# Queries, keys and recurrent inputs of the second mixer turned by transposing DMAs instead of TensorE

## The reference, cut to what matters

```python
def parallel_mixer(h, positions, w_in, conv_w, conv_b, w_rg, b_rg, w_ig, b_ig, lru_lambda, fox_b_f, w_out):
    proj = h @ w_in
    lx, ly, fq, fk, fv, ff, rq, rk, rv, rg = jnp.split(proj, np.cumsum(SPLIT_SIZES)[:-1].tolist(), axis=-1)
    lru_out = rg_lru(causal_depthwise_conv(lx, conv_w, conv_b), w_rg, b_rg, w_ig, b_ig, lru_lambda) * jax.nn.gelu(ly)
    fox_out = forgetting_attention(fq, fk, fv, ff, fox_b_f)
    ret_out = retention(rq, rk, rv, rg, positions)
    return jnp.concatenate([lru_out, fox_out.astype(h.dtype), ret_out], axis=-1) @ w_out

# in forgetting_attention, per head, with scale = HEAD_DIM ** -0.5:
logits = jnp.einsum('bhqd,bhkd->bhqk', qb, k).astype(jnp.float32) * scale + cb[..., None] - c[:, :, None, :]
```

## Time and profile before

| | us |
|---|---|
| runs | 2044.07, 2046.35, 2046.73 (median 2046.35) |
| span of the profiled execution | 2042.2 |
| PE busy | 2021.6 (99%) |
| DVE busy | 1410.4 (69%) |
| ACT busy | 1123.0 (55%) |
| mixer of the second block, layer 0, units 3 to 12 | 1235.6 to 1299.2 in the span |
| the same, layer 1 | 407.8 later |

### The profile page before, as it was taken

One profiled execution on the slowest core, in us unless ns is written; L12 is line 12 of the kernel. 1 busy time (PEld: TensorE's weight loads), 2 busy tenths in 40 slices (PEclk: granted clock), 3 DMA queues, 4 the chain that ended last, 5 costly groups with the idle time before them and its releaser, 6 DMA issues.

```text
span 2042.2 us, 24517 instructions
## 1 busy us (share of the span) xinstructions
PE 2021.6 (99%) x9754; PEld 1669.9 (82%) x9754; DVE 1410.4 (69%) x1855; ACT 1123.0 (55%) x1414; POOL 0.2 (0%) x4
## 2 busy tenths in 40 slices
PE   8999999999999999999999999999999999999998
PEld 6888887888888888887878888898888888988887
DVE  6666898776567556998776566856756658567565
ACT  6445667564445445666564446656544566565443
POOL 0000000000000000000000000000000000000000
PEclk9999999999999999999999999999999999999999
DMA  9776764567776775664567766444667654446764
GB/s 290 201 212 171 237 188 143 185 193 212 206 216 209 206 209 191 205 194 145 180 201 222 207 192 204 146 155 140 188 207 214 184 201 145 160 139 186 209 213 119
DMA packets 330226, 389.31 MB, mean 191 GB/s; under 512 B 102640, under 2 KB 238464, under 8 KB 330112
## 3 DMA queue, kind: packets, MB, share of 16 engines
q1 hardware_dynamic: 326016, 376.70, 60.5%
q10 hardware_dynamic: 4096, 11.05, 1.5%
HBM read 365.66 MB, written 1.05 MB: 180 GB/s over the span
## 4 chain that ended last, share of the span: by engine, by line
PE 95%; ACT 2%; DMA 2%; DVE 1%; issue 0%; SPq 0%; DVEq 0%; ACTq 0%
PE ps L584 85%; PE ps L1088 2%; PE ps L652 1%; PE ps L1191 1%; PE ps L1172 1%; DMA raw<-in_ffn_w_up 1%; PE ps L675 1%; ACT w_hi L1251 1%; PE ps L821 1%; DVE x L1869 0%; DMA raw<-in_w_in 0%; PE ps L1036 0%; PE ps L1002 0%; PE ps L727 0%; ACT scratch L1302 0%
## 5 line engine op out<-in xcount | busy, mean ns | idle before, releaser
L1829 DVE TENSOR_TENSOR w_lo<-raw,w_hi 128x2048 fp32r<-128x2048 f32 x338 | 772.4, 2289 | 268.9 <-ACT w_hi L1251 266.5
L1251 ACT ACTIVATE w_hi<-raw 128x2048 fp32r<-128x2048 f32 x342 | 648.5, 1897 | 458.6 <-PE ps L584 267.6
L584 PE MATMUL ps<-w_hi,hT_hi 128*128 128x512 f32 x2048 | 805.7, 393 | 1.4 <-DVE w_lo L1829 1.4
L584 PE MATMUL ps<-w_lo,hT_hi 128*128 128x512 f32 x2048 | 797.8, 390 | 0.0
L584 PE MATMUL ps<-w_hi,hT_lo 128*128 128x512 f32 x2048 | 775.4, 390 | 0.0
L584 PEld LDWEIGHTS ps<-w_hi,hT_hi 128*128 128x128 f32 x2048 | 384.6, 188 | 84.7 <-issue 5.5
L584 PEld LDWEIGHTS ps<-w_hi,hT_lo 128*128 128x128 f32 x2048 | 383.6, 188 | 79.9
L584 PEld LDWEIGHTS ps<-w_lo,hT_hi 128*128 128x128 f32 x2048 | 384.7, 188 | 76.9
L584 PE MATMUL ps<-w_hi,bT_hi 128*128 128x512 f32 x592 | 232.0, 392 | 0.5 <-DVE bT_lo L1910 0.5
L584 PE MATMUL ps<-w_lo,bT_hi 128*128 128x512 f32 x592 | 230.5, 389 | 0.0
L584 PE MATMUL ps<-w_hi,bT_lo 128*128 128x512 f32 x592 | 230.5, 389 | 0.0
(11 more groups left out here) (292 smaller groups left out, 1288.7 us busy)
## 6 DMA issues: line engine op xcount, KB each, us to landing
raw<-in_w_in SPq DMA_DIRECT2D x160, 512.0 KB, 4.6
raw<-in_ffn_w_gate SPq DMA_DIRECT2D x88, 512.0 KB, 4.0
raw<-in_ffn_w_up SPq DMA_DIRECT2D x88, 512.0 KB, 5.0
raw<-in_ffn_w_down SPq DMA_DIRECT2D x88, 512.0 KB, 4.3
raw<-in_w_gate SPq DMA_DIRECT2D x44, 512.0 KB, 4.0
raw<-in_w_up SPq DMA_DIRECT2D x44, 512.0 KB, 5.0
raw<-in_w_down SPq DMA_DIRECT2D x44, 512.0 KB, 4.2
raw<-in_w_out SPq DMA_DIRECT2D x32, 512.0 KB, 4.4
```

Of the source, the lines that this page charges most:

```text
L584: mm = nc.tensor.matmul(bank(t, half), act[:, tiles[i], t * P:(t + 1) * P], w, start=start and (i, n) == steps[0], stop=stop and (i, n) == ...
L1251: nc.scalar.activation(dst, src, ACT.Copy).then_inc(high_ready, 1)
L1829: V.tensor_tensor(lo, src, flat(hi), ALU.subtract).then_inc(low_ready, 1)
```

## The change

Queries, keys and x/y of the second mixer no longer pass through PE and PSUM. The rows that ACT wrote are split into planes by DVE (`fox_part`, `lru_part`), turned by two transposing DMAs each, and joined by DVE (`fox_join`, and two joins in `lru_conv`). The queries' factor 1/8 moves from ACT's copy into `rstd_eighth`, a small product on DVE. Planes and turned planes lie in tensors that are free at that time (`wide`, the upper half of `fvrT_f`, `vm`); the x/y planes reuse those of the queries. ACT's copies of the turned queries and keys are gone.

```diff
+                    if k == 9:
+                        sp.wait_ge(*after("fox_join", "q_planes", l))
+                        turn_planes(fq_planes_T, fq_planes, fox_q_turned)
+                    if k == 10:
+                        sp.wait_ge(*after("fox_join", "k_planes", l))
+                        turn_planes(fk_planes_T, fk_planes, fox_k_turned)
+                    if k == 12:
+                        sp.wait_ge(*after("lru_turn", "planes", l))
+                        turn_planes(lxy_planes_T, lxy_planes, lru_turned)
...
-        def fox_turn(l, which):
-            pe.wait_ge(*after("fox_in", which, l))
-            if which == "k":
-                pe.wait_ge(*after("fox_gate", "rows", l))
-            turn(fq if which == "q" else fk, 4 if which == "q" else 6).then_inc(*done("fox_turned", which))
-
-        def lru_turn(l):
-            pe.wait_ge(*after("lru_in", "xy", l))
-            pe.wait_ge(*after("fox_in", "qT", l))
-            turn(lxy, 4).then_inc(*done("lru_turned", "xy"))
...
-                pe.wait_ge(*after("fox_in", "kT", l))
+                pe.wait_ge(*after("fox_join", "k", l))
...
-            steps = {(1, 0): [fox_forget], (1, 1): [fox_decay, lambda l: fox_turn(l, "q")],
-                     (2, 1): [lambda l: fox_turn(l, "k")], (3, 1): [lru_turn, lambda l: fox_logits(l, 0)],
+            steps = {(1, 0): [fox_forget], (1, 1): [fox_decay], (3, 1): [lambda l: fox_logits(l, 0)],
...
-                       2: lambda: (act.wait_ge(*after("fox_turned", "q", l)), copy(fqT, two(4), "fox_in", "qT", 64 ** -0.5)),
-                       3: lambda: (act.wait_ge(*after("fox_turned", "k", l)), copy(fkT, two(6), "fox_in", "kT")),
...
+                if n == 0:
+                    act.wait_ge(*after("fox_join", "eighth", l))
+                if n == 4:
+                    act.wait_ge(*after("fox_join", "q", l))
...
+        def fox_part(l, which):
+            dve.wait_ge(*after("fox_in", which, l))
+            part_planes(fq_planes if which == "q" else fk_planes, fq if which == "q" else fk).then_inc(
+                *done("fox_join", which + "_planes"))
+
+        def fox_join(l, which):
+            dve.wait_ge(fox_q_turned if which == "q" else fox_k_turned, l * 32 + 32)
+            join_planes(*((fqT, fq_planes_T) if which == "q" else (fkT, fk_planes_T))).then_inc(*done("fox_join", which))
+
+        def lru_part(l):
+            dve.wait_ge(*after("lru_in", "xy", l))
+            part_planes(lxy_planes, lxy).then_inc(*done("lru_turn", "planes"))
+
         def lru_conv(l):
-            dve.wait_ge(*after("lru_turned", "xy", l))
-            V.tensor_copy(lxT[:, :, PAD2:PAD2 + T], two(4)[:, 0:2, :]).then_inc(*done("lru_turn", "x"))
-            V.tensor_copy(lyT.rearrange("p (c t) -> p c t", c=2), two(4)[:, 2:4, :]).then_inc(*done("lru_turn", "y"))
+            dve.wait_ge(lru_turned, l * 32 + 32)
+            src = lxy_planes_T.rearrange("p t (b c) n -> p t b c n", b=2)
+            join_planes(lxT[:, :, PAD2:PAD2 + T], src[:, :, :, 0:2, :]).then_inc(
+                *done("lru_turn", "x"))
+            join_planes(lyT.rearrange("p (c t) -> p c t", c=2), src[:, :, :, 2:4, :]).then_inc(*done("lru_turn", "y"))
...
+            V.tensor_scalar(rstd_eighth, rstd_in, 0.125, None, ALU.mult).then_inc(*done("fox_join", "eighth"))
             fox_gate(L)
             weight_low(L, 7)
+            fox_part(l, "q")
             fox_sums(l)
             weight_low(L, 8)
+            fox_part(l, "k")
             lru_lambda(l)
-            for k in (9, 10, 11, 12):
-                weight_low(L, k)
+            fox_join(l, "q")
+            weight_low(L, 9)
+            fox_join(l, "k")
+            weight_low(L, 10)
+            lru_part(l)
+            weight_low(L, 11)
+            weight_low(L, 12)
             lru_conv(l)
```

More of the change, by code:

```diff
@@ L300, in _program @@
     lxy = pairbuf.rearrange("p (t n) -> p t n", t=TT)
+    fq_planes, fq_planes_T = planes(wide[:, 0:1024]), planes_T(rT_f)
+    fk_planes, fk_planes_T = (w.rearrange("p m n -> p (m n)") for w in (vm[:, 0:1, :], vm[:, 1:2, :]))
+    fk_planes, fk_planes_T = planes(fk_planes), planes_T(fk_planes_T)
+    lxy_planes, lxy_planes_T = fq_planes, fq_planes_T
     ry_f, rsq_f = pairbuf[:, 0:512], pairbuf[:, 512:1024]
@@ L333, in _program @@
     conv_turned, gla_q_turned, sb_turned = sem("conv_u_turned"), sem("gla_q_turned"), sem("sb_qk_turned")
+    fox_q_turned, fox_k_turned, lru_turned = sem("fox_q_turned"), sem("fox_k_turned"), sem("lru_xy_turned")
     gT_hi_ready, gT_ready = sem("gT_hi_ready"), sem("gT_ready")
@@ L1382, in rows @@
         def rows(dst, src, stage, step, func=ACT.Copy):
-            scale = rstd_half if func == ACT.Tanh or step == "a" else rstd_eighth if (stage, step) == ("sb_in", "q") else rstd_in
+            scale = rstd_half if func == ACT.Tanh or step == "a" else rstd_eighth if step == "q" else rstd_in
             for t in range(TT):
@@ L2003, in join_planes @@
         def join_planes(dst, src):
+            if len(src.shape) == 4:
+                src = src.rearrange("p t (b c) n -> p t b c n", b=2)
             for t in range(TT):
                 joint = V.tensor_copy(dst.bitcast(U16).rearrange("p c (n b) -> p b c n", b=2)[:, :, :, t * P:(t + 1) * P],
-                                      src[:, t, :, :].rearrange("p (b c) n -> p b c n", b=2))
+                                      src[:, t, :, :, :])
             return joint
```

## The result

The changed kernel takes **2058.58 us** (median of 5 runs, 2055.41 to 2059.37), the kernel before 2046.73 in the runs beside it (2044.07 to 2047.78). The ratio is 1.0058, 95% interval 1.0048 to 1.0069: 11.85 us slower, where 10 had been forecast.

The account below looks back on a forecast made before the run. PE, busy 99% of the span, was taken as the bound: 2.6 us of turns spared per layer, but waits and clock loss leave each layer 5.0 us late; 2046.35 + 10 = 2056.4 us, range 2051.5 to 2062.

Parts of the forecast that it names:

- Steps 1 to 3: Layer 0, queries' and keys' splits, transposes and joins: unit 10 lands at 1266.3; first logits don't wait, 3 us spare.
- Step 4: Layer 0: x and y split behind unit 10's w_lo, planes at 1271.7; unit 12's load issued at 1274.4, landing at 1279.7.
- the bound of 6.3: Landings of units 10 and 12: at most 6.3 us, up to 1 us more each than the 5.3 used.
- Step 5: Layer 0: unit 12's w_lo, x and y joins, taps end at 1288.3; PE waits 5.9 us at the gates.
- the bound of twice that: DVE's joins of x and y could cost up to twice their neighbours, writing a padded tensor: 1.4 us more.
- The second wait: At the turned weights: sigmoids end 9.6 us after the last tap, so PE waits 1.3 us more.
- 0.45 us beyond the sigmoids for the clock: Behind the gates' wait: half clock loses PE 1.75 us, of which 1.3 were idle anyway, leaving 0.45 a layer.
- The turns are simply gained: Rival: unit 12's weights and planes come in time, nothing waits, 5.2 us gained, 2041.1 us; chance 0.04.
- The wait only eats the gain: Rival: path some 4 us shorter, PE waits about 2 us, kernel within 4 us of before, say 2048; chance 0.05.
- The milder loss: Rival: clock doesn't fall, landings short; 3.4 to 4 us a layer, 2053 to 2054.5 us; chance 0.15.
- The longer clock loss: Rival: clock stays low longer or falls twice a layer, another 1.75 us each, 2060 us; chance 0.13.
- I am wrong if unit 12's raw weights land before PE ends unit 10: Sign against the forecast that unit 12's load comes late and the gates wait about 5.9 us twice.

Follow-up runs that it names:

- the filler's run: Changed kernel plus 26 unread matmuls on PE ahead of its wait for the last tap, in both layers: 2057.53 us, ratio 1.0057 to the kernel before.
- the first experiment: Changed kernel with x and y's transposes behind unit 12's load in SP's list instead of ahead of it: 2041.65 us, ratio 0.9982 to the kernel before.
- x and y alone: Changed kernel with queries and keys turned by PE again, only x and y by DMA: 2045.07 us, ratio 0.9997 to the kernel before.
- the earlier split: Changed kernel with the split of x and y ahead of unit 10's w_lo in DVE's list: 2051.33 us, ratio 1.0032 to the kernel before.
- second profile: Changed kernel run once more, unaltered, beside the kernel with 26 unread matmuls: 2056.82 us, ratio 1.0057 to the kernel before.
- queries and keys by DMA: Changed kernel with x and y turned by PE again, only queries and keys by DMA: 2042.96 us, ratio 0.9986 to the kernel before.

## Why the prediction was right, and where a term was off

The changed profile's layer 0 starts 2.0 us later than in the earlier trace rows. The first units' matmuls show why: in the changed profile (first row) they start 0.43 us apart up to 17.1, in that of before (the other two rows) 0.23 us apart from 13.7 on.

```profile
14.15 0.63 PE L598 MATMUL ps<-w_lo,hT_hi 128*128 128x512 f32 x1
```

```profile
13.67 0.39 PE L584 MATMUL ps<-w_lo,hT_hi 128*128 128x512 f32 x1
13.90 0.40 PE L584 MATMUL ps<-w_hi,hT_hi 128*128 128x512 f32 x1
```

That makes about 1.8 us, and 0.2 us came from the first load. The granted clock of these stretches reads 1.00 in both profiles all the same, as it does for the 16 transposes of the earlier trace rows that the prediction took for half clock; so up to there the half rate is read from the lengths alone. I take 2.0 off all times of the changed profile.

**Steps 1 to 3 held.** The queries' split, 1253.7 for 1253.5; unit 9's load, 1256.3 for 1256.2. The keys' load of unit 10 was issued at 1261.8 for 1261.0: the second of the keys' transposes took 1.97 us to issue instead of 1.30. It landed at 1267.3 for 1266.3. Nothing waited at the first logits, as forecast.

**Step 4 was 1.7 us short in the end.** Split of x and y done at 1272.75 for 1271.7; unit 12's load issued at 1275.4 for 1274.4. It landed 6.0 us after its first DMA's issue, not 5.3: 1281.4 for 1279.7. That lies inside the bound of 6.3. Why it took longer isn't shown: six more issues followed at once, but in layer 1 the same six did, and the load landed in 5.4 us.

**Step 5 held in its lengths.** Four joins 1.38 us for 1.4 (the bound of twice that wasn't needed), taps 3.0. They end at 1290.0 for 1288.3, and PE came to the gates at 1282.4, as forecast. So the wait is **7.6 us where 5.9 stood**, 7.8 in layer 1. Of layer 0's 1.7 us, 0.2 arose in DVE's first splits, 0.65 in one transpose's issue, 0.2 in the landing of unit 10, 0.7 in that of unit 12. In layer 1 the keys' pair of transposes took 3.9 us to issue where 2.7 had been reckoned. These are the terms that were too small: the issue of one pair, and a landing.

**The second wait and the clock.** The sigmoids were to end 9.6 us after the last tap. In the changed profile ACT's row for them is at 1300.06 and 1.57 long, 1299.6 less the 2.0: just 9.6 behind the taps. PE came to the turned weights only at 1301.0, though, as it was slowed. So the wait of 1.3 us is never seen in the changed kernel; its place is taken by matmuls at half clock, as the prediction said it would overlap. The prediction had 0.45 us beyond the sigmoids for the clock, the four pairs of gates show 0.6 on the mean. The sigmoids' bound itself shows in the filler's run (9.69 us, waiting 1.2). Beside its sum the prediction names the section "HAM oscillation — how this bites in real kernels" of the Trainium skill's page "TensorE: Matmul & The Clock Gate", by which a rest between stretches of work is paid again in a warming-up. The trace agrees, in each of the four waits of the changed kernel seen, but the price here is mostly hidden: removing it (layer 0 with the filler) brought another bound to light.

**The sum.** In the profiles layer 0 loses 7.8 us and layer 1 6.1, where 5.0 each was forecast, and 1 us comes back at the end: 12.9, and 2.0 for the slower start, make the 14.9 between the spans. Layer 1 has 1.1 us of its lesser loss from somewhere else: in the profile of before PE waited there 0.8 us for DVE at an earlier step, and in the changed one it didn't.

```profile
PE ps L959 <- DVE scratch L2308: 0.8, 1, 0.8
```

So the forecast came as near as 1.85 us partly by luck: its path was short by more than that, and 2.1 us that were not in it, 1.1 in layer 1 and 1 at the end, came back outside of the path. The medians say 11.85 and 11.5. The 1.7 us of the late taps in two layers, 3.4, would have made 13.4 of the forecast's 10; the medians give half of this. The profile of before was its quickest execution (2044.07 against a median of 2046.73): each launch is 1.7 to 2.0 us longer than its own span, so more than half of the 4.15 us from span to median in the prediction was the spread of the executions. That of the changed kernel was one of its slower ones; so differences between these two traces come out larger than those of the medians. What the last 1.5 us are isn't settled.

**The rivals.** "The turns are simply gained" is what the changed kernel is not, but the first experiment comes near it by a single line: 3.4 us gained of the 5.2, the sigmoids' waits taking 2.3. (That 2041.65 lies so near the 2041.1 worked out is luck: the kernel before had 2046.35 for the one and 2045.06 beside the other.) "The wait only eats the gain" is what x and y alone do. "The milder loss" didn't come: the clock fell in every wait, and the landings of units 10 and 12 took 5.4 us or more. The longer clock loss did occur in length (the stretch at half clock is up to 10.3 us), but not in price. "I am wrong if unit 12's raw weights land before PE ends unit 10" marked the right place: that is what the first experiment brings about.

## What to carry to other kernels

A wait put into a queue's list is a wait for all that stands behind it there: look whose load comes next and who hangs on that, and if one may go ahead of it, put the wait one place later. Two such waits in one queue, each harmless, can be in series through the work that their loads feed (here load, high part, remainder, split, transpose, load), so cost them as one chain, and try them one without the other. And before paying to keep PE's clock up in a wait, look what is late next: here it was the sigmoids, and moving one instruction of ACT and one of DVE gave about 3 us, where 26 matmuls gave nothing that could be measured.

## What the runs showed of the hardware

- **Issuing a transposing DMA isn't of one length.** The keys' second transpose took 1.97 us of SP's queue in the changed kernel, where the queries' and x and y's took 1.30; in layer 1 it took 2.60. Its pair took 3.24 to 3.88 us in both layers of all seven profiles that have it, against 2.58 for the queries' pair. Unit 9's load, whose issues ended 1.1 us ahead of the pair, was in flight there. That this is the cause wasn't tried; with the earlier split x and y's pair came sooner behind a load, too, and took 3.18 us in layer 1, but 2.58 in layer 0.
- **A load's landing isn't of one length either.** Unit 12's load, 1 MB in two DMAs behind a pair of transposes, landed 6.0 and 5.4 us after its first issue in the two layers of the changed kernel, 5.9 and 5.6 in its second profile, and 7.2 and 6.2 with the earlier split. What sets it isn't shown.
- **The clock after a rest.** With the same filler ahead of it and rests of 1.96 and 2.03 us, the clock stayed at 1.00 in one layer and fell to 0.50 in the other. In the waits of 4.4 to 8.5 us (the changed kernel's two profiles and the earlier split) it fell 2.6 to 4.5 us after PE had stopped and rose 3.0 to 5.2 us after PE had begun again, with rests of 1.2 us and less (the first experiment) it stayed at 1.00. The stretches at half clock were from 3.4 to 10.3 us long, with the same work behind them.
- **One program, several starts.** By the lengths of the first units' matmuls, they ran at full rate from the first in four of the nine profiles, at half until 16.8 to 17.7 us in four, and in one they fell to half at about 14.7 us and came back at about 18.1, which there the granted clock shows too. In the changed kernel's profile all that follows lies 2.0 us later than in that of before. This is as much as the whole gain of queries and keys by DMA, so medians decide it and not two profiles.
